# Eight column tiles of layer 0's input product, taken by quarters of their rows between the modulation's units

## The chip, the cores and the metric

The kernel runs on one core of a Trainium2 chip. Its engines are TensorE (PE: matmuls into eight accumulator banks; PEld is its loading of stationary weights), VectorE (DVE), ScalarE (ACT), GpSimd (POOL) and SyncE (SP, which here only issues transfers). Each works through its own list of instructions in order and waits for the others by semaphores; sixteen DMA engines move the data. The metric is device time of one execution in microseconds (us).

## What is computed

Two blocks follow one another on a sequence of 256 positions with 2048 channels, batch 1. The change is in the first block, layer 0. Of the reference, what matters:

```python
c_act = jax.nn.silu(c)
for l in range(2):
    mod = c_act @ w_ada[l] + b_ada[l]                 # 2048 -> 6144
    shift, scale, gate = jnp.split(mod, 3, axis=-1)
    h = rms_norm(x, norm_g[l]) * (1.0 + scale[:, None, :]) + shift[:, None, :]
    proj = h @ w_in[l]                                # 2048 -> 6144, 256 positions
    u, z_s, q, k, v, z_a = jnp.split(proj, splits, axis=-1)
    y_s = s5_mixer(u, ...) * jax.nn.silu(z_s)         # state-space branch, then w_glu
    ...                                               # differential attention on q, k, v gives y_a
    x = x + gate[:, None, :] * (jnp.concatenate([y_s, y_a], axis=-1) @ w_out[l])
```

Row block k (128 channels) of h needs shift and scale of these channels only. The s5 branch needs u, the first 1024 columns of the product. The second block (w_in2, RWKV-7, MLA, a feed-forward part) stays as it is.

## The kernel before, in words

**Units and buffers.** All weights come in units of 1 MB (128 partitions by 2048 floats). A raw unit (w_ada) is read by TensorE as it is. A split unit is taken in two halves: for each, ScalarE writes the rounded high part (beat `hi`) and VectorE the rest (beat `lo`), and TensorE multiplies with both. Four such halves are held (`NS = 4`): rounding of half p waits until the product is through half p - 4. The units land in a ring, four buffers while only raw units are asked for (the fourth lies in what later holds K transposed), three after that. A transfer is issued on SyncE when the unit that had the buffer is done with: a raw one when TensorE has read it, a split one when its second half's `lo` is done.

**Blocks and tiles.** A block is 128 rows by 128 columns of a weight against 256 positions: three matmuls (high by high, high by low part of h, low by high). A column tile of w_in is 16 blocks that sum in one bank. The tiles of layer 0 are the eight of u (kind "u"), then 32 of q, k, v and z_a, then eight of z_s. An evicted u tile is written to memory by GpSimd (scr_u), and SyncE reads it back in another arrangement, eight transfers for each four tiles (`s5_u8`), for the s5 branch.

**The modulation.** 48 columns of 512 come as twelve column groups of four units for each layer. One unit costs TensorE four matmuls with 32 rows and 512 columns; after four of them ScalarE copies the row out (`modrow`), TensorE turns it into a column (`modend`, four matmuls 128 by 1), and VectorE adds the bias. The first eight groups of layer 0 (shift and scale, 32 units, in the order 0, 4, 1, 5, 2, 6, 3, 7) stand alone at the program's start. Group 4 + i gives the scale of rows 4i to 4i + 3; with it, the beats `gp` and `h` make that quarter of h. The other 16 groups (gate of layer 0, all of layer 1) stand between the blocks of the later products.

**What sets the order.** `Timeline.run` writes down one list of beats, and every engine's program is that list, filtered. `stream` walks the blocks of a product and lets the background generators take a turn after every `per` blocks: s5 (`self.s5`), the modulation (`g_mod`, which rests `mod_rest` turns after a unit), attention. A paced modulation gives out at most one raw unit for each split unit asked for (`raw_at`). Before glu the s5 generator is run to its end (`self.drain(g5)`), before layer 1 the modulation's. Before `stream` begins, all 32 first units are through:

```python
            self.mod_rest = 4
            self.stream("w_in", l, 48 * l, 0, 8, 16, per=4)
            ga = self.attention(l)
            self.bgs.append(ga)
            self.mod_rest = 8
            self.stream("w_in", l, 48 * l + 8, 8, 40, 16, per=2)
```

Of the kernel before, what the change touches and what calls it, by code (L numbers as in the profile page):

```python
# [12 lines left out]
ACT = mybir.ActivationFunctionType  # L13
# [264 lines left out]

PAIRS = (("w_in", 48), ("w_in2", 0), ("w_up", 0), ("w_pg", 0))


class Tile:


    def __init__(self, o, name, l, n, bank, before):
        self.o, self.name, self.l, self.n, self.bank, self.before = o, name, l, n, bank, before
        self.kind = "xf" if (name, l) == ("w_outm", 1) else kind_of(name, n)
        self.slots = {}


class Timeline:
    def __init__(self, units=None, plan=None):
        self.known, self.plan, self.order, self.asked = units, plan, [], 0
        self.raw_at, self.paced = -1, False
        self.units = []
        self.beats = []
# [14 lines left out]
        if units is not None:  # L311
            first = next(u for u, x in enumerate(units) if x[0] == "split")
            self.place = [u % 4 if u < first else u % NR for u in range(len(units))]
# [15 lines left out]
    def want(self, name, u):  # L329

        self.order.append((name, u))
        if self.plan is None:
            self.ask("split", name, u)
        while self.plan is not None and self.asked < min(len(self.order) + 1, len(self.plan)):
            self.ask("split", *self.plan[self.asked])
            self.asked += 1
# [79 lines left out]
    def follow(self, bank=None):  # L416
        for x in list(self.pend):
            if bank is None or x[0].bank == bank:
                while x in self.pend:
                    if next(x[1], self) is self:  # L420
                        self.pend.remove(x)
                    if bank is None:
                        break

    def ready(self, name, u0):

        for u in (u0, u0 + 1):
            self.want(name, u)
        self.split_ahead(self.halves + NS - 1)

    def stream(self, name, l, u0, n0, nt, nk, per=8, late=None):
# [3 lines left out]
        for blk in range(nt * nk):  # L435
# [6 lines left out]
            if blk % 8 == 0:  # L442
                p = self.halves
                self.halves += 1
                self.split_ahead(p + NS - 1)
                self.rest(p)
            if k == 0:
# [165 lines left out]
    def run(self):  # L613
# [13 lines left out]

        parts = 0
        for n, _ in enumerate(first):
            if n in (8, 9, 10, 11):  # L630
# [9 lines left out]
            while n >= 12 and ("mod", 0, 4 + parts) in self.marks:  # L640
                self.add("gp", 0, parts)
                for k in range(4 * parts, 4 * parts + 4):
                    self.add("h", 0, k)
                parts += 1
        self.split_ahead(NS - 1)
        self.banks = [0, 1, 2]
        gm = g_mod()
        self.paced = True
        for l in range(2):
# [14 lines left out]
            self.mod_rest = 4  # L664
            self.stream("w_in", l, 48 * l, 0, 8, 16, per=4)
            ga = self.attention(l)
            self.bgs.append(ga)
            self.mod_rest = 8
            self.stream("w_in", l, 48 * l + 8, 8, 40, 16, per=2)
# [276 lines left out]
def tensor_program(pe, m, tl, D):  # L946
    V, R, B, con = m.V, m.R, m.B, m.con

    def mm(t, k, p, b8):
# [6 lines left out]
        off = p % NS * 2 * HALF + b8 * 128  # L956
        o = B(t.bank, 0, 256, np_=M)
        pe.mm(o, R(off, M), r1, k == 0, False)
        pe.mm(o, R(off, M), r2, False, False)
# [342 lines left out]
def scalar_program(act, m, tl, D):  # L1302
# [251 lines left out]
    def ev(t, ph):  # L1554
# [4 lines left out]
        if t.kind == "u":  # L1559
            act.act(V(UT + 256 * n, (1, 32), (32, 8)), B(b, 0, 32, 8), ACT.Copy).then_inc("ev_act", key)  # L1560
        elif t.kind == "gate" and ph == 1:
# [906 lines left out]


def pack_ada(W):  # L2470

    b = W.reshape(4, 4, 128, 12, 512).transpose(3, 0, 2, 1, 4)
    return np.ascontiguousarray(b.reshape(48, 128, 2048))
# [9 lines left out]
def arrange(i):  # L2483
# [21 lines left out]
    order = np.concatenate([n, np.stack([16 + n, 24 + n, 32 + n, 40 + n], 1).reshape(-1), 8 + n])  # L2505
    A["w_in"] = np.concatenate([pack(w.reshape(2048, 48, 128)[:, order].reshape(2048, 6144)) for w in g["w_in"]])
    A["w_outm"] = np.concatenate([pack(w[:1024]) for w in g["w_out"]])
# [55 lines left out]
```

## Time and profile before

| | us |
|---|---|
| median of 3 runs | 3323.19 (3320.02 to 3326.16) |
| profiled execution | 3322.7 |
| its span in the trace | 3320.9 |
| TensorE matmuls busy in it | 3007.5 (91%) |
| VectorE busy | 2308.3 (70%) |
| ScalarE busy | 1640.0 (49%) |

The trace is of one execution. Rows of a timeline give start and length in us, the engine, the operation with its shape, and how many instructions were merged; brackets hold the idle time ahead of a row and what ended it. The page splits a matmul with fp32 operands into several records, so a modulation unit of four matmuls reads x8. Layer 0 of the first block ends near 800 us; the change acts in it.

### The profile page before, as it was taken

Reading aid. Unit: us, or ns where it says so; the run is one execution under the profiler, and the core shown is the slowest. Engines: PE = TensorE matmul, PEld = TensorE weight load, DVE = VectorE, ACT = ScalarE, POOL = GpSimd, SP = SyncE. Lnnn points to the kernel's source line nnn. Section 1 sums busy time; section 2 is a strip of 40 time slices with the busy share of each in tenths; the row PEclk is TensorE's granted clock in tenths of the full one; section 3 lists DMA queues with packets and bytes.
Section 4 is the critical chain, followed back from the end, with each engine's and each line's share of the span. In section 5 each row is a group of like instructions: output and inputs, shape, how many; then the busy total and the mean of one; then the engine's idle time right before and its main releaser. Section 6 shows DMA issues by size and latency. Waiting matters only on the chain.

```text
span 3320.9 us, 59768 instructions
## 1 busy us (share of the span) xinstructions
PE 3007.5 (91%) x24092; PEld 2772.4 (83%) x24092; DVE 2308.3 (70%) x3580; ACT 1640.0 (49%) x2416; POOL 323.9 (10%) x569
## 2 busy tenths in 40 slices
PE   6799898889998998999899999699899999999987
PEld 2587777768888888998888888689899999999987
DVE  6467776677688867775666665767588855887565
ACT  3345554345465644744444442455555544555454
POOL 0012222100122230200000000000000000000000
PEclk8799999889999998999999998899999999999999
DMA  9876656664644454454232232345445555554543
GB/s 371 291 250 219 224 210 238 237 229 173 176 137 139 139 159 166 169 191 157 93 110 93 98 106 79 132 139 187 151 156 180 189 190 179 179 189 166 186 149 123
DMA packets 110708, 576.93 MB, mean 174 GB/s; under 512 B 33056, under 2 KB 33088, under 8 KB 46688
## 3 DMA queue, kind: packets, MB, share of 16 engines
q1 hardware_dynamic: 89040, 525.37, 45.1%
q0 software_dynamic: 20816, 44.27, 4.6%
q8 instruction: 190, 3.11, 0.4%
q10 hardware_dynamic: 576, 3.47, 0.3%
q14 instruction: 86, 0.70, 0.1%
HBM read 546.83 MB, written 17.83 MB: 170 GB/s over the span
## 4 chain that ended last, share of the span: by engine, by line
PE 63%; DVE 23%; ACT 6%; DMA 4%; issue 3%; POOL 1%; SPq 0%; DVEq 0%; ACTq 0%; POOLq 0%
PE acc L872 62%; DVE arena L832 7%; DVE rounded L832 5%; DVE upper L832 2%; ACT arena L869 2%; DVE arena L842 2%; ACT rounded L869 2%; DMA arena<-in_w_ada 2%; DMA arena<-in_w_in 1%; DVE upper L842 1%; ACT upper L869 1%; DVE upper L850 1%; PE acc L875 1%; DVE rounded L842 1%; DVE arena L838 1%
## 5 line engine op out<-in xcount | busy, mean ns | idle before, releaser
L872 PE MATMUL acc<-rounded 128*128 128x256 f32 x14832 | 1953.8, 291 | 70.6 <-issue 43.9
L872 PEld LDWEIGHTS acc<-rounded 128*128 128x128 f32 x14832 | 1862.0, 196 | 152.8 <-issue 111.4
L832 DVE TENSOR_TENSOR rounded<-arena,rounded 128x1024 fp32r<-128x1024 f32 (+1 forms) x832 | 1005.3, 1208 | 334.0 <-ACT rounded L869 266.2
L869 ACT ACTIVATE rounded<-arena 128x1024 fp32r<-128x1024 f32 (+1 forms) x864 | 883.7, 1023 | 657.2 <-PE acc L872 502.6
L872 PEld LDWEIGHTS acc<-upper_rounded,rounded 128*128 128x128 f32 x4416 | 546.1, 197 | 40.5 <-DVE rounded L832 20.9
L872 PE MATMUL acc<-upper_rounded,rounded 128*128 128x256 f32 x4416 | 553.8, 289 | 18.6 <-DVE rounded L832 18.5
L869 ACT ACTIVATE arena<-arena 128x256 f32<-128x256 f32 (+4 forms) x469 | 248.9, 531 | 302.6 <-DVE arena L832 210.9
L872 PE MATMUL acc<-arena 128*32 128x512 f32 (+7 forms) x1874 | 272.2, 475 | 88.8 <-DVE arena L832 46.3
L832 DVE TENSOR_TENSOR arena<-arena 128x256 f32<-128x256 f32 (+6 forms) x519 | 273.2, 526 | 52.0 <-ACT arena L869 30.3
L872 PEld LDWEIGHTS acc<-arena 128*32 128x32 f32 (+4 forms) x1874 | 126.0, 143 | 152.9 <-DMA arena<-in_w_ada 63.0
L842 DVE SCALAR_TENSOR_TENSOR arena<-arena 128x256 f32<-128x256 f32 (+5 forms) x461 | 205.7, 446 | 42.7 <-ACT arena L869 14.5
L832 DVE TENSOR_TENSOR arena<-acc,arena 128x256 f32<-128x256 f32 (+3 forms) x280 | 119.1, 425 | 162.3 <-PE acc L872 144.3
L869 ACT ACTIVATE arena<-acc 128x256 f32<-128x256 f32 (+4 forms) x284 | 119.0, 419 | 224.6 <-PE acc L872 207.6
L872 PE MATMUL acc<-upper 128*128 128x128 f32 (+9 forms) x1632 | 195.5, 298 | 9.5 <-DVE upper L832 4.8
L872 PEld LDWEIGHTS acc<-upper 128*128 128x128 f32 (+4 forms) x1632 | 155.3, 169 | 35.0 <-issue 12.8
L828 POOL DMA_DIRECT2D arena<-arena x256 | 130.4, 517 | 422.0 <-ACT arena L869 415.2
L869 ACT ACTIVATE upper<-acc 128x256 f32<-128x256 f32 (+4 forms) x176 | 88.2, 501 | 158.1 <-PE acc L872 106.8
L872 PE MATMUL acc<-upper,arena 64*64 64x64 f32 (+3 forms) x546 | 88.9, 356 | 42.5 <-DVE upper L832 26.6
L869 ACT ACTIVATE arena<-acc,arena 128x256 f32<-128x256 f32 (+1 forms) x154 | 66.3, 430 | 100.7 <-PE acc L872 92.8
L872 PEld LDWEIGHTS acc<-upper,arena 128*128 128x128 f32 (+2 forms) x546 | 57.8, 173 | 61.6 <-DVE upper L832 30.1
L875 PE MATMUL acc<-arena 128*128 128x128 f32 x384 | 73.0, 285 | 28.0 <-ACT arena L869 22.6
L869 ACT ACT_TABLE_LOAD x70 | 89.8, 1283 | 8.4 <-issue 3.1
(88 smaller groups left out, 1137.0 us busy)
## 6 DMA issues: line engine op xcount, KB each, us to landing
arena<-in_w_in SPq DMA_DIRECT2D x164, 1024.0 KB, 5.0
arena<-in_w_ada SPq DMA_DIRECT2D x88, 1024.0 KB, 5.2
arena<-in_w_up SPq DMA_DIRECT2D x88, 1024.0 KB, 4.8
arena<-in_w_down SPq DMA_DIRECT2D x44, 1024.0 KB, 4.8
arena<-in_w_outa SPq DMA_DIRECT2D x16, 1024.0 KB, 7.0
arena<-in_w_glu SPq DMA_DIRECT2D x16, 1024.0 KB, 5.3
arena<-in_w_outm SPq DMA_DIRECT2D x16, 1024.0 KB, 5.1
arena<-in_w_out SPq DMA_DIRECT2D x16, 1024.0 KB, 4.9
```

Of the source, the lines that this page charges most:

```text
L828: self.e.dma_start(out, in_).then_inc(self.signals.sems[sem], 16)
L832: return self.put(self.e and self.e.tensor_tensor(o, a, b, op))
L838: return self.put(self.e and self.e.tensor_scalar(o, a, s1, s2, o1, o2))
L842: return self.put(self.e and self.e.scalar_tensor_tensor(out=o, in0=a, scalar=s, in1=b, op0=o1, op1=o2))
L850: return self.put(self.e and self.e.reciprocal(o, a))
L869: return self.put(self.e and self.e.activation(o, a, f, scale=scale, **kw))
L872: return self.put(self.e and self.e.matmul(o, l, r, start=start, stop=stop, skip_group_check=True))
L875: return self.put(self.e and self.e.transpose(o, i, self.m.con("ident")))
```

## The change

The eight u tiles of layer 0 are no longer a stream of their own behind the modulation. A generator `early` takes them by quarters of the rows: as soon as a quarter of h is written down, it asks for two split units that hold the 4 row blocks of all eight tiles, and it lays six blocks behind each of the modulation's units. Eight sums are open at once: tile n and tile n + 4 share bank n % 4 (bank 7 stands for the fourth), at columns 0 and 256, and only the first matmul of the lower one clears the bank. The last quarter has an order of its own, tiles 0, 1, 4, 5, 2, 3, 6, 7. A tile of the lower half is evicted when its neighbour has ended too. The host packs these eight units by quarters. The ring keeps four buffers until these units are through. The first stream and its 32 turns for the background go away in layer 0, and the rest of the modulation in the second stream is 7 turns in place of 8.

```diff
-PAIRS = (("w_in", 48), ("w_in2", 0), ("w_up", 0), ("w_pg", 0))
+PAIRS = (("w_in", 6), ("w_in", 48), ("w_in2", 0), ("w_up", 0), ("w_pg", 0))
...
-            first = next(u for u, x in enumerate(units) if x[0] == "split")
+            first = next(u for u, x in enumerate(units) if x == ("split", "w_in", 8))
...
-        while self.plan is not None and self.asked < min(len(self.order) + 1, len(self.plan)):
+        while self.plan is not None and self.asked < min(len(self.order) + self.ahead, len(self.plan)):
...
+    def early(self):
+
+        for n in range(8):
+            b = self.banks[n % 4]
+            t = Tile(n, "w_in", 0, n, b, None)
+            t.nk, t.at = 16, 256 * (n // 4)
...
+        for q in range(4):
+            while ("h", 0, q) not in self.marks:
+                yield
+            if q == 3:
+                self.ready("w_in", 6)
+            else:
+                self.want("w_in", 2 * q)
+                self.split_ahead(self.halves + NS - 1)
+                self.rest(self.split - 1)
+                yield
+            for h, first in enumerate((0, 2, 4, 6) if q < 3 else (0, 4, 2, 6)):
+                p = self.half()
...
+                for b8 in range(8):
+                    self.add("mm", self.tiles[first + b8 // 4], 4 * q + b8 % 4, p, b8)
+                    if q < 3 and (8 * h + b8) % 6 == 5:
+                        yield
...
+            next(ge, None)
+        for _ in ge:
+            pass
+        self.ahead = 1
...
-            self.stream("w_in", l, 48 * l, 0, 8, 16, per=4)
+            if l:
+                self.stream("w_in", l, 48 * l, 0, 8, 16, per=4)
             ga = self.attention(l)
             self.bgs.append(ga)
-            self.mod_rest = 8
+            self.mod_rest = 7
...
-        o = B(t.bank, 0, 256, np_=M)
-        pe.mm(o, R(off, M), r1, k == 0, False)
+        o = B(t.bank, t.at, 256, np_=M)
+        pe.mm(o, R(off, M), r1, k == 0 and t.at == 0, False)
...
+            if t.beside is not None:
+                act.wait_ge("mm", ("out", t.beside.o))
```

What this moves, engine by engine. TensorE's list where the modulation's second scale group is under way, before (32x512 is a unit, 128x1 a column's end, upper a buffer of the ring; 128x256 from rounded is the product, three to a block):

```order
L872 MATMUL acc<-upper,arena 128x4
L872 MATMUL acc<-arena 32x512 x8
L872 MATMUL acc<-arena 128x1 x4
L872 MATMUL acc<-upper,arena 32x512 x4
L872 MATMUL acc<-arena 32x512 x12
L872 MATMUL acc<-arena 128x1 x4
L875 MATMUL acc<-arena 128x128 x4
```

The same place now:

```order
L924 MATMUL acc<-upper,arena 128x4
L924 MATMUL acc<-arena 32x512 x4
L924 MATMUL acc<-rounded 128x256 x18
L924 MATMUL acc<-upper,arena 32x512 x4
L924 MATMUL acc<-arena 128x1 x4
L924 MATMUL acc<-rounded 128x256 x18
L924 MATMUL acc<-arena 32x512 x4
L924 MATMUL acc<-rounded 128x256 x18
L924 MATMUL acc<-arena 32x512 x4
L924 MATMUL acc<-rounded 128x256 x18
```

Six blocks stand behind each unit from the second unit of group 5 on; nothing of the product stood there before.

TensorE's list behind the eighth tile, before (the last 12 matmuls of it are the first row; 32x128 and 128x128 are matmuls of the s5 branch):

```order
L872 MATMUL acc<-rounded 128x256 x12
L872 MATMUL acc<-arena,upper 32x128 x4
L872 MATMUL acc<-arena 32x128 x4
L872 MATMUL acc<-rounded 128x256 x12
L872 MATMUL acc<-arena 128x1 x4
L872 MATMUL acc<-rounded 128x256 x6
L872 MATMUL acc<-arena 32x512 x4
```

Now (of the 108 the last 6 are tile 8's; the row with 32x128 reads the reloaded u):

```order
L924 MATMUL acc<-rounded 128x256 x108
L924 MATMUL acc<-arena 32x512 x4
L924 MATMUL acc<-rounded 128x256 x30
L924 MATMUL acc<-arena,upper 32x128 x4
L924 MATMUL acc<-rounded 128x256 x18
L924 MATMUL acc<-arena 32x512 x4
```

Before, the unit stood 6 blocks into tile 8; now it stands 2 blocks into it, and the next one, 10 + 6 blocks later, 2 blocks into tile 9. The reading of u has moved from the middle of the eight tiles to 12 blocks behind them.

VectorE's list at the end of w_outa in layer 0, before (rounded 128x1024 is a rounding of weights, arena<-acc the eviction of a tile, upper_rounded the last step of a finished row block of s5, 128x8 the first instruction for w_glu):

```order
L842 SCALAR_TENSOR_TENSOR upper<-arena,upper 128x256
L832 TENSOR_TENSOR rounded<-arena,rounded 128x1024
L832 TENSOR_TENSOR upper_rounded<-upper,upper_rounded 128x256
L842 SCALAR_TENSOR_TENSOR arena<-acc,arena 128x256
L842 SCALAR_TENSOR_TENSOR upper<-arena,upper 128x256
L832 TENSOR_TENSOR rounded<-arena,rounded 128x1024
L832 TENSOR_TENSOR upper_rounded<-upper,upper_rounded 128x256
L842 SCALAR_TENSOR_TENSOR arena<-acc,arena 128x256
L832 TENSOR_TENSOR rounded<-arena,rounded 128x1024
L842 SCALAR_TENSOR_TENSOR arena<-acc,arena 128x256
L837 TENSOR_SCALAR arena<-arena 128x8
L832 TENSOR_TENSOR rounded<-arena,rounded 128x1024 x2
```

Now:

```order
L890 TENSOR_SCALAR arena<-arena 128x256
L884 TENSOR_TENSOR arena<-arena,upper 128x256
L894 SCALAR_TENSOR_TENSOR upper<-arena,upper 128x256
L884 TENSOR_TENSOR upper_rounded<-upper,upper_rounded 128x256
L894 SCALAR_TENSOR_TENSOR upper<-upper,arena 128x256
L884 TENSOR_TENSOR arena<-upper 128x256
L890 TENSOR_SCALAR arena<-arena 128x256
L884 TENSOR_TENSOR arena<-arena,upper 128x256
L894 SCALAR_TENSOR_TENSOR upper<-arena,upper 128x256
L884 TENSOR_TENSOR upper_rounded<-upper,upper_rounded 128x256
L894 SCALAR_TENSOR_TENSOR upper<-arena,upper 128x256
L884 TENSOR_TENSOR upper_rounded<-upper,upper_rounded 128x256
L889 TENSOR_SCALAR arena<-arena 128x8
L884 TENSOR_TENSOR rounded<-arena,rounded 128x1024 x2
```

Three steps of s5 (s5_out and the row block that it finishes) stand directly ahead of w_glu with no rounding and no eviction between them; before, two tiles of w_outa followed the last of them.

## Rows read from the trace of the kernel before

**Rows 1.** The page's head; then windows, TensorE to DMA, of layer 0

```profile
span 3320.9 us, 59768 instructions
...
core 0: us, PE busy (x) PEld busy (x) DVE busy (x) ACT busy (x) POOL busy (x), PEclk, DMA share, GB/s
57.00:111.00 54.00, 36.05 (x213) 12.71 (x212) 28.89 (x75) 17.42 (x31) 4.60 (x9) 0.71 0.95 370
111.00:184.00 73.00, 63.53 (x490) 52.77 (x490) 30.91 (x34) 25.73 (x30) 4.36 (x8) 0.89 0.76 256
184.00:590.00 406.00, 375.81 (x3149) 309.65 (x3146) 293.06 (x507) 214.90 (x393) 91.59 (x172) 0.97 0.66 227
```

**Rows 2.** Timeline of TensorE: start, us, operation, [idle before it], 95 to 184

```profile
111.34 0.77 PE L872 MATMUL acc<-rounded 128*128 128x256 f32 x2 [5.49 <-ACT rounded L869]
112.51 2.50 PE L872 MATMUL acc<-rounded 128*128 128x256 f32 x10 [0.40 <-DVE rounded L832]
...
124.02 6.01 PE L872 MATMUL acc<-rounded 128*128 128x256 f32 x48
...
144.86 0.95 PE L872 MATMUL acc<-arena 128*128 128x1 f32 x8
...
160.53 0.65 PE L872 MATMUL acc<-arena,upper 128*32 128x128 f32 x8 [7.69 <-DMA upper<-scr_u]
...
181.81 1.67 PE L872 MATMUL acc<-rounded 128*128 128x256 f32 x12
```

**Rows 3.** Timeline of VectorE, 63 to 96: s5 step, tables, a quarter of h

```profile
63.00 1.55 DVE L832 TENSOR_TENSOR arena<-arena 128x576 f32<-128x576 f32 x2
...
64.92 0.29 DVE L846 CAST upper<-upper 128x256 f32<-128x256 int32 x1
...
90.69 0.16 DVE L842 SCALAR_TENSOR_TENSOR arena<-arena 128x4 f32<-128x4 f32 x1
...
94.22 1.07 DVE L842 SCALAR_TENSOR_TENSOR rounded<-upper,arena,rounded 128x256 fp32r<-128x256 f32 x2
```

**Rows 4.** Timeline of ScalarE and VectorE: four roundings of weights

```profile
110.14 4.39 ACT L869 ACTIVATE rounded<-arena 128x1024 fp32r<-128x1024 f32 x4
...
111.23 5.21 DVE L832 TENSOR_TENSOR rounded<-arena,rounded 128x1024 fp32r<-128x1024 f32 x4 [0.55 <-ACT rounded L869]
```

**Rows 5.** The page's transfers: w_ada's units, us to landing at the end

```profile
arena<-in_w_ada SPq DMA_DIRECT2D x88, 1024.0 KB, 5.2
```

**Rows 6.** Waits of TensorE, 184 to 590 (us in total, times, longest), and two units

```profile
PE acc L872 <- DMA arena<-in_w_ada: 13.0, 5, 5.1
PE acc L875 <- ACT arena L869: 12.6, 7, 3.4
...
503.18 1.94 PE L872 MATMUL acc<-arena 128*32 128x512 f32 x8 [2.74 <-DMA arena<-in_w_ada]
...
539.50 1.94 PE L872 MATMUL acc<-arena 128*32 128x512 f32 x8 [5.12 <-DMA arena<-in_w_ada]
```

**Rows 7.** ScalarE evicts tile 3; SyncE issues the reload of u

```profile
143.63 0.64 ACT L869 ACTIVATE upper<-acc 128x256 f32<-128x256 f32 x1 [1.77 <-PE acc L872]
...
148.90 7.95 SPq L828 DMA_DIRECT2D upper<-scr_u  x8
```

**Rows 8.** One unit's way: ScalarE, VectorE, SyncE, TensorE, 442 to 451

```profile
442.44 1.06 ACT L869 ACTIVATE rounded<-arena 128x1024 fp32r<-128x1024 f32 x1 [4.11 <-PE acc L872]
...
444.63 1.23 DVE L832 TENSOR_TENSOR rounded<-arena,rounded 128x1024 fp32r<-128x1024 f32 x1
...
445.88 0.33 SPq L828 DMA_DIRECT2D arena<-in_w_ada  x1
...
450.76 1.06 PE L872 MATMUL acc<-arena 128*32 128x512 f32 x8 [3.28 <-DMA arena<-in_w_ada]
```

**Rows 9.** VectorE in w_outa: where two s5_out steps begin

```profile
620.69 0.48 DVE L842 SCALAR_TENSOR_TENSOR upper<-upper,arena 128x256 f32<-128x256 f32 x1
...
625.74 0.48 DVE L842 SCALAR_TENSOR_TENSOR upper<-upper,arena 128x256 f32<-128x256 f32 x1
```

**Rows 10.** TensorE at the end of layer 0: the norm's matmul

```profile
799.68 0.70 PE L872 MATMUL acc<-arena 128*128 128x256 f32 x2 [1.64 <-DVE arena L832]
```

## What the change does to the time: the prediction

> **What bounds the kernel now.** The windows come first [rows 1]. Over the whole span TensorE is the engine that is nearly always busy; the reader is to see where it is not. From 57 to 111 us its matmul column shows 36 of 54 us, and half of that at the low clock (granted 0.71): the first 32 units of the modulation arrive at 370 GB/s, DMA share 0.95. So that stretch is bounded by transfers. From 111 to 184 us the eight tiles run, 63.5 of 73 us busy at only 256 GB/s: bounded by TensorE. The change fills one stretch with the work of the other. From 184 to 590 us (column tiles 8 to 47) TensorE is 93% busy.
>
> The timeline of TensorE [rows 2] gives prices. The product's first matmul starts at 111.34. After an idle stretch it runs at 0.25 us (x10 in 2.50, the level of 1.2 GHz), later at 0.125 us (x48 in 6.01, 2.4 GHz). A block is three of them, 0.376 us, 48.2 us for 128 blocks. A unit of the modulation costs 1.03 us (1.06 less overlap), a column's end 0.85. At 160.53 TensorE has sat 7.69 us for the reload of u (scr_u). The last matmuls of tile 7 end at 183.5.
>
> **Part 1: the eight tiles under the modulation.** Rows of h are ready in quarters. The first is done when VectorE turns to the next step, at 63.0; a quarter takes 4.6 us from gp to its last row (90.69 to 95.29) [rows 3]. Rounding the first half of a weight unit takes ScalarE 1.1 us and VectorE 1.3 [rows 4], and the first is rounded directly behind the quarter: the first blocks can run whole at 64.7. From there TensorE has 128 blocks (48.2), 18 units (18.5), six column ends (5.1) and 1.6 of s5 matmuls: 73.4 us. Waits on top: a quarter of h cannot start before its scale column is in, and TensorE stands behind it in order. That leaves 2.5, 1.5 and 4.0 us at the second, third and last quarter (4.6 less what TensorE still has queued). Three transfers are gated by a rounding or by the unit before them in their buffer and are late by about 2 us each, a landing being 5.2 us from issue [rows 5]: 5.3. Sum 64.7+73.4+13.3 = 151.4. The low clock returns after idle stretches of 2.7 us and more (the 1.94 us unit at 503.18 [rows 6]); I add 3.6, since part of what a slow stretch loses is taken from the next wait. Stage end: **155**, with 151 and 165 as the ends. Transfers do not bind: the eight units are 8.4 MB, 23 us at the 370 GB/s of [rows 1], and 111+23 is still ahead of 155. VectorE's tables, which begin at 64.92 [rows 3], now stand behind four roundings (5.2 us) and ahead of the fifth; they are over before the second quarter's column is in, at about 85.
>
> What is late next is the reload of u. Before, it landed 16.9 us after tile 3's last matmul: its eviction follows at 143.63, and eight transfers are issued from 148.90 on, one per us [rows 7]. Now tile 3 ends with the stage, and TensorE has 12 blocks and one unit, 5.6 us, ahead of the matmul that reads it. So this wait grows from 7.7 to 11.3 us, and the reader is reached at 155+16.9 = 171.9. To compare with 183.5: still to be done are 7 units (7.3), a column end (0.85) and s5 matmuls (1.6); the restart at the low clock costs 2.5; 12 blocks (4.5) are already done. 171.9+9.7+2.5-4.5 = 179.6. **Gain 3.9 us**, 8 at the near end, and 6 lost at the far one.
>
> TensorE: Matmul & The Clock Gate in the Trainium skill says in its section on HAM oscillation that a TensorE which waits for transfers between short stretches of work keeps falling back to the low clock and pays for warming each time. The trace agrees for the unit behind 2.74 us (1.94 us, at 503.18) and not for the one behind 3.28 us (1.06, at 450.76); with every wait of this stage charged at 2.5 the stage would end near 166.
>
> **Part 2: where the later units stand.** This is what the diff hides. With a rest of 8 turns the unit of a column tile wandered: at tile 8 it stood 6 blocks into its tile, two blocks later with each column, until it was a tile behind. With 7 turns it is always ready early and is held by the pacing rule (one unit per weight unit), so all 32 units of tiles 8 to 39, and those of 40 to 47, stand two blocks into their tile. The transfer is issued when a rounding frees the buffer, and that rounding waits for a fixed block of the product. Counting blocks (0.376), units and s5 and attention matmuls between that block and the reading unit gives, for tiles 8 to 47, 9.8 to 18.5 us before with a mean of 13.8, and 8.2 to 12.6 with a mean of **10.6** now; under 10.7 us stand 5 of 38 before and 26 of 39 now. What is needed: 1.1 + 1.3 for the rounding, 5.2 for the landing, and VectorE's lag, as [rows 8] show it from 443.5 (ScalarE done) to 444.63. Over the forty issues from 184 to 590 the same pair of rows gives lags from 0.0 to 5.9, mean 2.4. So need is 7.6 plus lag. The unit at 450.76 is one that already stood two blocks in, and it waited 3.28 [rows 8]. Laying the forty lags against the distances gives 24 us of waits now against 5 by the same arithmetic before, where the trace shows 13.0 in five [rows 6]. The difference, 19, is the upper end; while TensorE waits, VectorE catches up, and the 12.6 us of waits for ScalarE in the same tiles partly disappear. The lower end is 0. I take two thirds, **+12 us**, low clock included, because the row at 450.76 is the nearest.
>
> DMA: Bandwidth & Descriptors in the Trainium skill (Anatomy of one DMA) gives about 2.0 us plus bytes over 436 GB/s, an estimate of 4.4 us for this transfer. The trace's median is 5.2 [rows 5]; by the page the waits would be some 8 us fewer.
>
> **Part 3: the end of s5.** The s5 generator loses the 32 turns of the first stream, so it ends later in w_outa. Nine s5_out steps run at 5.05 us each (620.69 to 625.74 [rows 9]), longer than the 3.0 us of blocks beside them, so VectorE bounds there. Before, they start behind tile 5 of 16; now behind tile 10, and the last three stand with nothing of the product beside them. Five more tiles come first and cost TensorE 15.1 plus two units, 17.2. In return the chain sheds the roundings and evictions of five tiles (1.3 + 0.5 each, 8.8) and the tile and a half that followed its end (4.5). Net +4. Distances of units in w_outa and w_glu fall from a mean of 11.9 to 9.2 us; half of that is hidden under VectorE's bound: +2. At the end of layer 0 the last unit, its row and column end now stand ahead of the norm's matmul, where TensorE waited 1.64 us [rows 10]: 1.06 and 0.85 and ScalarE's copy of the row between them take its place, +1. Together **+7**.
>
> **The copy, the bank with two sums, the packed rows** cost nothing: the matmuls and the weight units are the same in number and size; an eviction of a low tile waits for its neighbour, which ends 1.5 us later. If that cover were gone it would be 0.7 us four times.
>
> **Sum**, against the profiled execution (3322.7, its span 3320.9, median of the three 3323.19): 3322.7 - 3.9 + 12 + 7 = 3337.8, rounded down to 3337.
>
> **The rivals.**
> A, faster: the later waits do not grow, since most lags are under 3 us and TensorE's own waits let VectorE catch up. Then 3322.7 - 8 (stage end 151) - 3 (the waits that the wandering caused, such as 5.12 us at 539.50 [rows 6]) + 0 = 3312. It decides if waits for in_w_ada between tiles 8 and 47 stay under 13 us and s5 finds the room it needs. For: a 72% busy VectorE. Against: [rows 8].
> B, no change: part 1 as forecast, part 2 at +3, part 3 at +4: 3326.
> C, much slower: the stage itself is long. TensorE is in order, so each wait for h or for a weight also holds back the units behind it and their buffers, four at the time, and with them the transfers. Stage end 165, part 1 becomes a loss of 6: 3348.
> D, the change does not do what it says, in that blocks stand between units but only wait there: the product would end no earlier than with all rows ready at 126 and 128 blocks behind it, 174: 3357. I give it little, since rows of h are ready from 63.
>
> **How the numbers follow.** Forecast (3330 to 3345) 0.47, A 0.20, B 0.20, C 0.10, D 0.03. A measurement of this kernel can tell about 0.2%, 6.6 us, from no change. B is within it, with its ends shared out evenly. Faster 0.20, same 0.20, slower 0.60. The range leaves out half of A and half of C with D: 3313 to 3352.
>
> **What would show it.** First rounded matmul near 64; tile 7's last near 155 (C: 165); a wait for scr_u of about 11 us behind it; from there to tile 47 waits for in_w_ada of 25 us or so in more than ten places (A: under 13, in five); between w_outa and w_glu an idle stretch of TensorE of some 8 us. The forecast is wrong if the distances count for less than the lags suggest, or if the low clock stays away from the first stage.

## The result, and the profile after

| | before | changed |
|---|---|---|
| median of 4 runs (us) | 3322.08 (3320.02 to 3326.16) | 3372.71 (3370.55 to 3380.64) |
| ratio | | 1.0155 (95% interval 1.0136 to 1.0175) |
| profiled execution's span | 3320.9 | 3378.8 |
| end of layer 0's product (last matmul before the norm) | 798.0 | 850.9 |

The kernel is 50 us slower, where 3337 was forecast. The last row of the table is counted in the traces: layer 0 of the first block ends 52.9 us later. What lies behind it, where the lists are the same, takes from 2508 to 2529 us over all the traces here, in no order that follows the edits; so layer 0's end is the cleaner measure of a single trace below. It isn't exact either, for each kernel has one trace: kernels whose lists are the same up to tile 7 end it at 183.0 to 184.0 us, and the interleaved ones with six blocks per unit at 159.8 to 163.4. The profiled execution of the changed kernel is the slowest of its four (3380.64 us).

The windows of the changed kernel, to be laid beside [rows 1]; columns as there:

```profile
span 3378.8 us, 59767 instructions
...
57.00:111.00 54.00, 45.16 (x321) 31.88 (x324) 26.63 (x53) 17.50 (x24) 0.54 (x1) 0.87 0.75 296
111.00:184.00 73.00, 56.86 (x383) 45.23 (x383) 33.40 (x52) 28.15 (x38) 9.08 (x17) 0.81 0.80 243
184.00:590.00 406.00, 357.53 (x2883) 289.89 (x2882) 278.56 (x486) 205.69 (x376) 81.21 (x157) 0.93 0.59 207
590.00:800.00 210.00, 158.40 (x1189) 131.57 (x1188) 127.50 (x232) 75.94 (x107) 21.42 (x37) 0.88 0.60 213
```

The stretch that the change fills is fuller, as meant: TensorE is busy for 45.2 us from 57 to 111, against 36.1. But from 184 to 590, where the diff changes one number, it is busy for 357.5 us against 375.8, and does only 2883 matmul records against 3149. A record takes 124.0 ns there against 119.3, at a granted clock of 0.93 against 0.97: besides standing idle, it also runs slower, by 2883 x 4.7 ns = 13.5 us.

TensorE's timeline at the two ends of the eight tiles (start, length, operation, idle before it and what ended it), as in [rows 2]:

```profile
63.65 0.77 PE L924 MATMUL acc<-rounded 128*128 128x256 f32 x2 [5.55 <-ACT rounded L921]
...
147.93 16.16 PE L924 MATMUL acc<-rounded 128*128 128x256 f32 x102 [0.78 <-DVE rounded L894]
...
175.89 0.66 PE L924 MATMUL acc<-arena,upper 128*32 128x128 f32 x8 [6.21 <-DMA upper<-scr_u]
```

The product starts at 63.65 (forecast 64), but its eighth tile ends at 163.4 (forecast 155; the last 6 of these 102 matmuls are tile 8's), and the reloaded u is read at 175.89 (forecast 171.9).

TensorE's waits for in_w_ada in the changed kernel, first from 184 to 590, then from 590 to 800 (us in total, times, longest); [rows 6] has 13.0, 5, 5.1 for the first, and before shows 11.6, 5, 3.3 in the second:

```profile
PE acc L924 <- DMA arena<-in_w_ada: 44.2, 16, 5.6
...
PE acc L924 <- DMA arena<-in_w_ada: 42.1, 14, 9.3
```

Those two rows are 31 + 31 us more of waiting for modulation units, more than the whole loss of 52.9. The 13.5 us of slow matmuls come on top; what the first stage gains and what other waits give up (those for ScalarE's results in these tiles fall from 12.6 to 0.5 us) goes off. One unit's way, to compare with [rows 8] (ScalarE rounds a half of a weight unit, VectorE its low part, SyncE issues, TensorE reads):

```profile
352.93 1.06 ACT L921 ACTIVATE rounded<-arena 128x1024 fp32r<-128x1024 f32 x1
...
361.68 1.23 DVE L884 TENSOR_TENSOR rounded<-arena,rounded 128x1024 fp32r<-128x1024 f32 x1
...
362.93 0.33 SPq L880 DMA_DIRECT2D arena<-in_w_ada  x1
...
367.77 1.94 PE L924 MATMUL acc<-arena 128*32 128x512 f32 x8 [4.49 <-DMA arena<-in_w_ada]
```

ScalarE is done at 353.99; VectorE comes to the low part at 361.68, 7.7 us later, because steps of s5 and attention stand ahead of it in its list; the landing takes 4.8 us. The unit itself runs at 1.94 us, the level of 1.2 GHz. TensorE: Matmul & The Clock Gate in the Trainium skill says (HAM oscillation) that short stretches between waits pay for warming again and again. The trace agrees here, behind 4.49 us, and not at 685.82, where a unit behind 3.24 us takes 1.06.

### The profile page after: what moved, and what is told of

It reads as the page before. It is cut to its first block, busy times and chain, and to the rows that moved or that the text cites. A ratio compares the mean times of both kernels' runs of the same rounds, so it can differ in the third digit from the quotient of the medians.

```text
span 3378.8 us, 59767 instructions
## 1 busy us (share of the span) xinstructions
PE 3023.1 (89%) x24092; PEld 2786.0 (82%) x24092; DVE 2308.3 (68%) x3580; ACT 1642.5 (49%) x2418; POOL 321.2 (10%) x569
## 4 chain that ended last, share of the span: by engine, by line
PE 61%; DVE 23%; DMA 6%; ACT 6%; issue 3%; POOL 0%; DVEq 0%; SPq 0%; ACTq 0%; POOLq 0%
PE acc L924 61%; DVE arena L884 7%; DVE rounded L884 5%; DMA arena<-in_w_ada 3%; DVE upper L884 2%; DVE arena L894 2%; ACT arena L921 2%; ACT rounded L921 2%; DVE upper L894 1%; ACT upper L921 1%; DVE rounded L894 1%; DVE upper L902 1%; PE acc L927 1%; ACT L921 1%; DVE arena L890 1%
## 5 line engine op out<-in xcount | busy, mean ns | idle before, releaser
L924 PE MATMUL acc<-rounded 128*128 128x256 f32 x14832 | 1974.8, 293 | 73.5 <-issue 43.5
L924 PEld LDWEIGHTS acc<-upper 128*128 128x128 f32 (+4 forms) x1632 | 155.0, 168 | 34.2 <-issue 11.4
```

The source lines that it names most:

```text
L924: return self.put(self.e and self.e.matmul(o, l, r, start=start, stop=stop, skip_group_check=True))
```

## The experiments

Each ratio is to the kernel before on the same chip, run again beside each group of experiments: its medians there were 3320.97 us (the first four), 3326.61 (the next four) and 3324.00 (the last four). So kernels of different groups are compared by their ratios and not by their microseconds. Two theories stood at the start. **P** (place): the units cost what they cost because they stand too close behind the rounding that frees their buffer. **V** (VectorE): s5 stands later in VectorE's list, ahead of other roundings, and in a lump at the end of w_outa.

### Place or VectorE

b_units_held is the kernel before with one number changed:

```diff
-            self.mod_rest = 8
+            self.mod_rest = 7
```

> The kernel before with one number changed: the later modulation units rest 7 turns in place of 8 from column tile 8 on, so they are held by the pacing rule and stand two blocks into their tile, as in the changed kernel; the first eight tiles and the order of s5 stay as they were. Theory P (place: what costs is that the unit stands too close behind the rounding that frees its buffer): TensorE waits for in_w_ada between 184 and 590 us rise from 13 us to 30 us or more, and the time from 3322 to 3340 to 3355 us. Theory V (VectorE: what costs is that the s5 steps stand later, ahead of other roundings, and in a lump at the end of w_outa): s5 hasn't moved, so 3320 to 3328 us.

Measured: 3369.73 us, ratio 1.0144 (1.0125 to 1.0162). It is by itself nearly the whole of the change's 1.0155. Layer 0 ends at 853.2 us, 2.3 later than in the changed kernel. Its waits for in_w_ada from 184 to 590 and from 590 to 800:

```profile
PE acc L872 <- DMA arena<-in_w_ada: 46.0, 18, 7.0
...
PE acc L872 <- DMA arena<-in_w_ada: 50.8, 12, 8.7
```

Theory V's forecast (no change) falls, and P's own figure, 3340 to 3355, was too low.

a_units_late is the changed kernel with the units four turns later in their tile (ten blocks in rather than two), up to tile 47:

```diff
                 while self.paced and len(self.order) == self.raw_at:
                     yield "wait"
+                for _ in range(self.mod_late if self.paced else 0):
+                    yield "wait"
...
-            self.mod_rest = 7
+            self.mod_rest, self.mod_late = 3, 4
...
+            self.mod_late = 0        # ahead of w_outa
```

> The changed kernel with the later modulation units standing four turns (eight blocks of the product, 3.0 us) later in their tile, ten blocks in, from column tile 8 to 47; everything else as it is. The distance between the rounding that frees the buffer and the reading unit grows from a mean of 10.6 to 14.4 us there; w_outa and w_glu are untouched. Theory P: the 48 us of waits for in_w_ada in these tiles fall below 12 us, and the time from 3372 to 3335 to 3345 us. Theory V: the roundings are as late as before, the waits move to other places, 3362 to 3375 us.

Measured: 3331.73 us, ratio 1.0034 (1.0019 to 1.0048): 41 us of the 50 are back, with the waits of these tiles where P had them, the time 3 us below P's range, and far from V's. The waits of tiles 8 to 47 are gone, those of w_outa and w_glu are not:

```profile
PE acc L928 <- DMA arena<-in_w_ada: 5.4, 4, 2.8
...
PE acc L928 <- DMA arena<-in_w_ada: 37.6, 13, 8.5
```

a_s5_early gives s5 its 32 turns back and leaves the units where they are:

```diff
+        def more():
+            while ("u8", 0, 0) not in self.marks:
+                yield
+            for n in range(32):
+                next(g5, None)
+                for _ in range(2):
+                    yield
...
-                self.bgs += [g5, gm]
+                self.bgs += [g5, gm, more()]
```

> The changed kernel with the s5 generator given 32 extra turns, one after every second ordinary turn from the reload of u on, so that it stands in w_outa where it stood before or a little earlier (first s5_out at block 786 of the product; 816 before the change, 850 in the changed kernel). The units stay two blocks into their tile. Theory P: the waits for in_w_ada in tiles 8 to 47 stay near 48 us; w_outa gets back some 12 us of its 20: 3358 to 3364 us. Theory V: waits fall in w_in too: 3335 to 3350 us.

Measured: 3372.57 us, ratio 1.0156 (1.0139 to 1.0173), the same as the changed kernel's 1.0155. The 12 us that P allowed for w_outa did not come either: the waits for in_w_ada are still 40.1 us in 14 places from 590 to 800, and w_outa takes 93.4 us against 91.0. The one trace does end layer 0 at 842.8, 8 us before the changed kernel's; the times of the executions don't show it.

a_late_and_s5 has both edits, with the units late in w_outa too.

> The changed kernel with both: units four turns later in their tile from tile 8 to the end of w_outa, and the 32 extra turns for s5. If place and the lump of s5 are separate costs, their gains add: 3372 less some 34 less some 14, 3318 to 3332 us. If either theory alone is right, the time is that of its own run: near 3340 (P) or near 3342 (V), with nothing from the other.

Measured: 3312.70 us, ratio 0.9968 (0.9949 to 0.9987). Better than the sum that was expected, but it holds a third edit (w_outa), so it doesn't say which of them paid. The next runs take that apart.

### w_outa, and part 1 alone

a_late_outa is a_units_late with the later place kept to the end of w_outa (`self.mod_late = 0` moved behind it), and s5 as in the changed kernel.

> As the changed kernel with its units four turns later (3331.7 us), but later in w_outa too; s5 stands where the changed kernel has it. From block 768 to 896 of the product that kernel takes 95.3 us against 79.6 before. If it is the units' place there (distance 8 to 9 us behind the freeing rounding), some 12 of these 16 us come back: 3318 to 3323 us. If it is the lump of s5 at the end of w_outa, the time stays at 3328 to 3334 us.

Measured: 3312.36 us, ratio 0.9956 (0.9940 to 0.9972). So the place in w_outa was worth 0.78%, some 26 us by the ratios and 20.7 by the ends of layer 0 in the traces (808.3 and 787.6), more than expected. The 32 turns of s5 were worth nothing that could be measured: with them 0.9968, without them 0.9956, and layer 0 ends at 788.5 and 787.6 us. They save 7.1 us in w_outa and w_glu (162.5 us without, 155.4 with them, blocks 768 to 1024 of the product). Tiles 8 to 47 take 8.3 us more with them, at a lower granted clock (0.95 against 0.98 from 184 to 590); in the pair of kernels with four blocks per unit below, where that clock is 0.97 in both, it is 3.1 us.

b_units_late is the kernel before, with its eight u tiles as a stream of their own, and the same late units:

> The kernel before, its eight u tiles a stream of their own, with the later modulation units held and ten blocks into their tile from tile 8 to the end of w_outa: all that the kernel with both edits (3312.7 us) has, without the interleaving of the first eight tiles. What lies between the two is part 1 alone. By the first eight tiles' ends, corrected for the units done by then, part 1 gains 5 to 7 us: 3317 to 3321 us here. If the interleaving gains nothing once the waits behind it are gone, 3311 to 3315 us; if it is the 20 us that the end of tile 7 shows uncorrected, 3330 us.

Measured: 3309.70 us, ratio 0.9942 (0.9925 to 0.9959), below all three expected ranges. The interleaving of the first eight tiles gains nothing on the whole: 0.9956 with it, 0.9942 without, intervals that overlap. The ends of blocks in the two traces show where it goes. From block 160 to block 1024 the changed order has done 8 units and 2 column ends fewer (8 x 1.03 + 2 x 0.85 = 9.9 us), which the third column takes off. At block 128 it is one column end less (9.1 us), and at block 1152 only half a unit and a column end are left (1.4 us):

| end of product block | b_units_late | a_late_outa | lead of a_late_outa, corrected |
|---|---|---|---|
| 128 (tile 7) | 183.9 | 160.1 | 14.7 |
| 160 (tile 9) | 202.3 | 185.0 | 7.4 |
| 768 (last of w_in) | 584.5 | 566.1 | 8.5 |
| 896 (last of w_outa) | 661.0 | 636.8 | 14.3 |
| 1024 (last of w_glu) | 741.4 | 728.6 | 2.9 |
| 1152 (last of layer 0) | 789.6 | 787.6 | 0.6 |

The first stage wins 14.7 us, the reload of u takes half of it back at once, w_outa wins 5.8, and w_glu takes 11.4. There s5's last steps stand beside nothing of the product. That this is s5's place can be seen with the 32 turns: a_late_and_s5 takes 79.3 us for w_glu against 91.8, but 76.1 for w_outa against 70.7. ScalarE's timeline in a_late_outa, then TensorE's:

```profile
640.61 0.51 ACT L924 ACTIVATE arena<-arena 128x256 f32<-128x256 f32 x1 [3.01 <-DVE arena L887]
641.21 0.60 ACT L924 ACTIVATE arena<-acc 128x512 f32<-128x512 f32 x1
...
641.86 1.77 PE L927 MATMUL acc<-arena 128*128 128x1 f32 x8 [5.05 <-ACT arena L924]
...
650.43 0.63 PE L927 MATMUL acc<-upper_rounded,rounded 128*128 128x256 f32 x3 [0.97 <-DVE upper_rounded L887]
651.88 6.42 PE L927 MATMUL acc<-upper_rounded,rounded 128*128 128x256 f32 x39 [0.82 <-DVE upper_rounded L887]
```

The copy of the modulation's row (641.21) stands on ScalarE behind a step of s5_out that waits for VectorE, and TensorE's column end waits 5.05 us for the copy; at the same place b_units_late shows 0.81.

c_reader_late is a_late_and_s5 with eight more turns ahead of the first step that reads the reloaded u.

> The changed kernel with both edits (units four turns later, 32 extra turns for s5), and the first step that reads the reloaded u eight turns later: 22 blocks behind the eighth tile in place of 12. The wait for scr_u, 6 to 9 us there, gets 3.8 us more of cover. If TensorE stands only for the reload, 3308 to 3310 us. If s5, later by as much, gives it back in w_outa, 3311 to 3316 us.

Measured: 3319.61 us, ratio 0.9981 (0.9967 to 0.9996). The cover works where it stands (block 160 ends at 180.6 instead of 185.2), and it is given back: block 768 ends at 583.3 instead of 574.1. It is no better than 0.9968, and 3319.61 us lies above both expected ranges.

c_four_blocks is a_late_and_s5 with `% 4 == 3` for `% 6 == 5` in `early`.

> The changed kernel with both edits, and four blocks of the product behind each modulation unit of the first stage instead of six, so that a quarter's 32 blocks are spread over eight units. If tile 7 ends late (160 to 163 us, 155 forecast) because the transfers come in bursts, gated by units that wait behind blocks, the stage ends 3 to 5 us earlier: 3308 to 3310 us. If TensorE's own work and the roundings set the end, it doesn't move: 3311 to 3315 us.

Measured: 3311.55 us, ratio 0.9949 (0.9929 to 0.9969). Tile 7 ends at 162.3 us, not earlier than at 159.8 with six blocks, so the number of blocks per unit is not what makes the stage late. The bunch of transfers that it was meant to thin out was still there: the last of them is issued at 129.80 us, as against 129.58 in the changed kernel.

### How the cost depends on the place

Two more kernels are the one before with held units at other places, everything else as in b_units_late:

```diff
-            self.mod_rest, self.mod_late = 3, 4
+            self.mod_rest, self.mod_late = 5, 2      # b_six_blocks_in; 1, 6 in b_fourteen_blocks_in
```

> The kernel before with its later modulation units held, six blocks into their tile (two turns later than held at two; to the end of w_outa). Mean distance from the freeing rounding to the reader 12.4 us in tiles 8 to 47, against 10.6 when held at two blocks (3370 us) and 14.4 at ten (3310 us). Laying the delays of ScalarE and VectorE that the trace of before shows for its own units against these distances gives 32 us of waits there and 60 in w_outa and w_glu, 26 more than at ten blocks and 49 fewer than at two. Theory P, with the delays as measured: 3325 to 3340 us, nearer the far end of the row than the middle. If it is the mere regularity of the units, in phase with the tiles, that costs, and not the distance: 3355 us or more.

Measured: 3327.37 us, ratio 1.0009 (0.9996 to 1.0022), inside P's range.

> The same with the units fourteen blocks into their tile, mean distance 16.2 us. By the same arithmetic 4 us of waits are left in tiles 8 to 47 where 11 stand at ten blocks, and 44 in w_outa and w_glu where 56 stand. Theory P: a gain that runs out, 3298 to 3310 us. If a longer hold of the buffer makes the split units' transfers late instead, 3312 to 3325 us.

Measured: 3311.76 us, ratio 0.9961 (0.9944 to 0.9978), between the two ranges. The gain has run out at ten blocks already.

With two of the kernels above this is a curve. The distance is counted in the lists from the block that lets the freeing rounding begin to the unit that reads; the waits are for in_w_ada:

| blocks into the tile | mean distance, tiles 8 to 47 | waits 184 to 590 | waits 590 to 800 | ratio |
|---|---|---|---|---|
| 2 (b_units_held) | 10.6 us | 46.0 | 50.8 | 1.0144 |
| 6 | 12.4 | 22.9 | 33.3 | 1.0009 |
| 10 (b_units_late) | 14.4 | 7.0 | 21.2 | 0.9942 |
| 14 | 16.2 | none | 23.6 | 0.9961 |
| wandering (before) | 13.8 | 13.0 | 11.6 | 1 |

Four blocks (1.5 us and what stands between) are worth 45 us at first, then 22, then nothing. The units are held in phase with the tiles in all four, so it is not the regularity that costs. The last step is not clear in the traces: with fourteen blocks layer 0 ends at 801.6 us and with ten at 789.6, though the waits for in_w_ada are no longer.

The row that explains it is one unit in both ends of the curve, the one of tile 27. Held at two blocks:

```profile
370.78 1.06 ACT L869 ACTIVATE rounded<-arena 128x1024 fp32r<-128x1024 f32 x1
...
380.61 1.23 DVE L832 TENSOR_TENSOR rounded<-arena,rounded 128x1024 fp32r<-128x1024 f32 x1
...
381.87 0.33 SPq L828 DMA_DIRECT2D arena<-in_w_ada  x1
...
386.70 1.94 PE L872 MATMUL acc<-arena 128*32 128x512 f32 x8 [3.90 <-DMA arena<-in_w_ada]
```

The same unit at ten blocks:

```profile
363.28 1.07 ACT L872 ACTIVATE rounded<-arena 128x1024 fp32r<-128x1024 f32 x1
...
373.70 1.22 DVE L835 TENSOR_TENSOR rounded<-arena,rounded 128x1024 fp32r<-128x1024 f32 x1
...
374.95 0.33 SPq L831 DMA_DIRECT2D arena<-in_w_ada  x1
...
380.00 1.04 PE L875 MATMUL acc<-arena 128*32 128x512 f32 x8
```

VectorE is late by 8.8 us (371.84 to 380.61) in the one and 9.4 us (364.35 to 373.70) in the other, the transfer takes 4.8 and at most 5.0. Nothing on the way got quicker; the reader only stands 17 us behind the start of the rounding rather than 12.

b_glu_too keeps the units two turns late in w_glu as well.

> The kernel before with units ten blocks into their tile to the end of w_outa (3309.7 us), and two turns (eight blocks) later in w_glu as well. In w_glu one unit waits 8 to 9 us for its transfer in every kernel so far, since its buffer's rounding stands behind VectorE's first steps for the second layer's s5. With 3 us more of distance: 3302 to 3308 us. If w_glu is bounded by VectorE there and the wait only moves: 3308 to 3312 us.

Measured: 3307.88 us, ratio 0.9962 (0.9949 to 0.9975). The longest wait for in_w_ada from 590 to 840 falls from 8.4 to 3.5 us and layer 0 ends at 787.1 instead of 789.6, but the ratio isn't better than 0.9942: no gain that could be measured.

a_late_four_blocks is a_late_outa with four blocks per unit in the first stage.

> The changed kernel with its units ten blocks into their tile to the end of w_outa (3312 us) and four blocks of the product behind each unit of the first stage, s5 where the change puts it. The run with four blocks and the s5 turns ended its first stage no earlier (162.3 us) and gave the ratio 0.9949 to the kernel before, against 0.9968 with six. If blocks per unit don't matter: 3310 to 3314 us. If waits are spread better at four: 3304 to 3309 us.

Measured: 3313.42 us, ratio 0.9961 (0.9944 to 0.9978), with layer 0's end at 790.2. The time doesn't show that blocks per unit matter.

The best that ran is b_units_late, 0.9942: it beats both kernels, and it leaves the first eight tiles alone. That it is better than the others with late units isn't shown, since their intervals overlap with its own. The size of its gain is open too: 0.58% is 19 us, but the trace ends layer 0 only 8.4 us before that of the kernel before.

## Why the prediction was wrong

**The direction was right, and so was the place of the later units as the largest cost; its size was not.** Part 2 was put at +12 us, with 19 as its upper end, and a further +2 in part 3 for the same thing in w_outa and w_glu. b_units_held measures both together, 14 us forecast: +48 us in the median (1.0144), 55 in the trace's layer 0. Of these 55, tiles 8 to 47 take 30.5 and w_outa 26.0 (w_glu 2.7; 3.7 come back behind it). What else the change does is small, as forecast (-3.9 and +5): the changed kernel's ratio is 0.11% above that of b_units_held, within the intervals.

**The step that failed** is "what is needed: 7.6 plus lag, mean 2.4". Two things were wrong in it. First, the lags, taken as 0.0 to 5.9 us, were read off the wrong pairs of rows. [rows 8] lays VectorE's rounding at 444.63 beside ScalarE's at 442.44, but VectorE was further behind than that. VectorE's two roundings ahead of it, and ScalarE's last one ahead of 442.44:

```profile
431.00 1.23 DVE L832 TENSOR_TENSOR rounded<-arena,rounded 128x1024 fp32r<-128x1024 f32 x1 [1.31 <-ACT rounded L869]
...
436.90 1.06 ACT L869 ACTIVATE rounded<-arena 128x1024 fp32r<-128x1024 f32 x1
...
437.54 1.23 DVE L832 TENSOR_TENSOR rounded<-arena,rounded 128x1024 fp32r<-128x1024 f32 x1
```

VectorE's rounding at 431.00 waited for ScalarE's of 429.91, which ends at 430.97, and both engines go on in the same order. So VectorE's at 437.54 belongs to ScalarE's at 433.11, and the one at 444.63 to ScalarE's at 436.90: the unit at 450.76 had a lag of 6.7 us and not of 1.1. Pairing each transfer's two roundings by their number in the lists, the trace of before gives for the 38 units of tiles 8 to 47 lags up to 10.5 us with a mean of 3.3, five of them over 6. Second, the rounding doesn't begin when its half is free: ScalarE starts it 1.3 us later on average (at least 0.5), a term that the sum didn't have. Together: 1.3 + 1.1 + 3.3 + 1.2 + 4.9 (the landing) = 11.8 us, more than the 10.6 us of mean distance, where 10.0 had looked just enough. Laid against the distances, these figures of before give 72 us of waits held at two blocks, and 24 for before; with the wrong ones it had been 24 and 5. About 0.6 of it is what the traces show (46.0 of 72 and 13.0 of 24), so "I take two thirds" was sound, and it was applied to the wrong number. That before showed 13.0 us where the arithmetic gave 5 was the sign; it should have been followed up before the 24 was believed. The landing was not the step that failed. The fit that the prediction lays beside it, from DMA: Bandwidth & Descriptors in the Trainium skill (Anatomy of one DMA), is given there for transfers on the GpSimd path, and the units are issued by SyncE; it entered no sum.

**A second term was hardly sized**: "low clock included" was one phrase. The windows of before and the changed kernel differ by 13.5 us in it, those of before and b_units_held by 7.9 (2933 records at 122.0 ns). That it is the price of these waits isn't shown: from 184 to 590 us b_six_blocks_in waits 22.9 us for in_w_ada at 117.5 ns a record and a granted clock of 0.99, a_late_and_s5 1.5 us at 122.4 ns and 0.95.

**w_outa was passed over.** A mean distance of 9.2 us in w_outa and w_glu was priced at +2, "half hidden under VectorE's bound". It cost some 26 us (a_units_late against a_late_outa by the ratios; 26.0 in w_outa in the traces of b_units_held and before), and the trace shows VectorE's bound at work: with s5_out steps ahead of the roundings the lags there are 14.0, 9.3 and 8.3 us for the units at blocks 834, 850 and 866 of the changed kernel. Here the engine that bounds the stage doesn't hide a transfer that it gates; it delays it. The longest wait there, 8.54 us at 649.48, is another: its transfer took 10.2 us to land.

**Part 1** (-3.9) came out in its sum by luck: the stage ended 8 us late (163.4), the wait for the reload was 5 us shorter, and what is left of the two is no larger than the 3 us by which traces with the same lists differ. Corrected for the 9.9 us of units, block 160 ends 3.9 us earlier in the changed kernel than in b_units_held (197.2 against 201.1), and 7.4 us earlier in a_late_outa than in b_units_late; less than 1 us of either is left at the end of layer 0. But the stage ended at 160 to 163 us in all the kernels that have it, not at 155. "Transfers do not bind" failed. SyncE's issues (start, length, operation) and what waits for their landing:

```profile
113.81 0.33 SPq L880 DMA_DIRECT2D arena<-in_w_in  x1
123.00 0.33 SPq L880 DMA_DIRECT2D upper<-in_w_ada  x1
123.37 2.23 SPq L880 DMA_DIRECT2D arena<-in_w_ada  x2
126.03 0.33 SPq L880 DMA_DIRECT2D arena<-in_w_in  x1
129.58 0.33 SPq L880 DMA_DIRECT2D upper<-in_w_in  x1
...
139.50 1.06 ACT L921 ACTIVATE rounded<-arena 128x1024 fp32r<-128x1024 f32 x1 [14.08 <-DMA arena<-in_w_in]
...
142.00 1.06 ACT L921 ACTIVATE rounded<-upper 128x1024 fp32r<-128x1024 f32 x1 [1.44 <-DMA upper<-in_w_in]
143.15 0.60 ACT L921 ACTIVATE arena<-acc 128x512 f32<-128x512 f32 x1
...
143.80 1.87 PE L924 MATMUL acc<-arena 128*128 128x1 f32 x8 [4.34 <-ACT arena L921]
```

Nothing is issued between 113.8 and 123.0, since the buffers are held by units whose work waits for the third quarter of h (VectorE's next rounding stands behind the last row, from 121.74 to 122.97, and the issue follows); then five units in 7 us. Five MB at the 370 GB/s of [rows 1] take 14 us, and the last lands 12.4 us after its issue. The average rate of the stage said that there was room; the issues are bunched (340 GB/s from 123 to 142 us, DMA share 0.95). ScalarE, in order, waits for that weight ahead of the copy of the modulation's row, and TensorE for the copy. This chain is read from the trace; no run removed it. The reload's wait was 6.2 us rather than 11.3, because u landed 12.5 us behind the end of the stage and not 16.9: tile 3 ends 2.9 us before the stage (160.5), and SyncE issues the eight transfers in 4.0 us (from 167.58) where it took 8.0 in [rows 7]. Reader and gain came out within 4 us of the forecast.

**Part 3** (+7): the idle stretch of some 8 us between w_outa and w_glu did not appear. Its waits were 2.83, 2.26 and 0.44 us. The likely reason, which no run isolates, is that with TensorE waiting for units all along VectorE had caught up:

```profile
707.60 1.55 PE L924 MATMUL acc<-arena 128*32 128x512 f32 x8 [2.83 <-DMA arena<-in_w_ada]
...
713.04 1.01 PE L924 MATMUL acc<-upper_rounded,rounded 128*128 128x256 f32 x3 [2.26 <-DVE upper_rounded L884]
714.49 6.58 PE L924 MATMUL acc<-upper_rounded,rounded 128*128 128x256 f32 x39 [0.44 <-DVE upper_rounded L884]
```

With the units out of the way a loss shows, the 11.4 us in w_glu by which a_late_outa falls back behind b_units_late. Giving s5 its turns back only moved it, to w_outa and the tiles before. Why layer 0 ends between 786 and 790 us in six of the eight kernels with units ten blocks or more into the tile up to w_outa, whatever else they do (c_reader_late 798, b_fourteen_blocks_in 802), was not isolated.

**The rivals.** C (0.10) had the stage's end nearly right (165) and its consequence wrong; A and B fell with the 44 us of waits. No rival had the units' place as costly as it is. Theory P, in the first expectations, still underpriced it (3340 to 3355), for it used the same wrong lags.

## What to carry to other kernels

Where a buffer's release hangs on an engine that also does other work, price the whole chain (start of the releasing step, its queue, its length, the transfer) for every instance from the trace, and look at the tail of that sum, not its mean: here a reader held at too short a distance met every late case, and four blocks more or less (two or six) decided over 1.35%. If the same arithmetic does not reproduce the waits that the trace already shows, it isn't ready to be used on the change. And when a change moves a background schedule, try the schedule alone first: here a single number, apart from the idea it came with, was nearly the whole loss, and holding the same units later was all the gain that any run found.

## What was not expected of the hardware

Waits of about 3 us don't always end in the low clock, though the prediction let it return behind 2.7 us and more: a unit behind 2.74 us took 1.94 us before [rows 6], one behind 3.28 took 1.06 [rows 8], and in the changed kernel one behind 3.34 us took 1.06 at 696.16 while one behind 3.90 us took 1.94 in b_units_held.
